# Hybrid retention and attention encoder layer with routed experts: order of the first expert weight blocks, residual input loaded elsewhere, and activations placed ahead of a weight split

## The reference

```python
def gated_merge(x, y_r, y_d, gr, gd, w_out):
    m = jax.nn.sigmoid(gr) * y_r + jax.nn.sigmoid(gd) * y_d
    return x + jnp.einsum('btd,de->bte', m, w_out)

def hier_moe(h, w_group, b_group, w_expert, b_expert, w_gate, w_up, w_down):
    ...
    for e in range(N_EXPERTS):
        he = jax.nn.silu(xt @ w_gate[e]) * (xt @ w_up[e])
        y = y + combine[:, e:e + 1] * (he @ w_down[e]).astype(F32)
    return y.reshape(B, T, D).astype(h.dtype)
```

## Time and profile before

| | us |
|---|---|
| median of 3 runs | 1039.63 (1039.24 to 1040.72) |
| profiled execution, its own time | 1038.06 |
| its span in the trace | 1036.2 |
| outside the span | 1.9 |
| mean granted TensorE clock | 0.996 |

### The profile page before, as it was taken

One profiled execution on the slowest core, in us unless ns is written; L12 is line 12 of the kernel. 1 busy time (PEld: TensorE's weight loads), 2 busy tenths in 40 slices (PEclk: granted clock), 3 DMA queues, 4 the chain that ended last, 5 costly groups with the idle time before them and its releaser, 6 DMA issues.

```text
span 1036.2 us, 12524 instructions
## 1 busy us (share of the span) xinstructions
PE 1011.0 (98%) x4814; PEld 834.1 (80%) x4814; DVE 679.0 (66%) x999; ACT 529.3 (51%) x728; POOL 149.8 (14%) x185
## 2 busy tenths in 40 slices
PE   7999999999999999999999999999999999999996
PEld 6888888887888878778778888888878888888774
DVE  6877765236566564344438556678799888888982
ACT  5433333435555555233352213455677877868772
POOL 1000020112111302111112000021121211212102
PEclk9999999999999999999999999999999999999998
DMA  9258855362542614432457433238899999999994
GB/s 302 83 193 302 306 202 193 126 242 94 192 164 91 207 59 162 163 113 106 168 183 265 151 107 134 102 107 317 316 422 384 404 382 404 394 393 404 382 391 65
DMA packets 62421, 237.69 MB, mean 229 GB/s; under 512 B 5632, under 2 KB 5936, under 8 KB 50032
## 3 DMA queue, kind: packets, MB, share of 16 engines
q1 hardware_dynamic: 41328, 162.80, 41.1%
q0 software_dynamic: 21024, 73.99, 21.6%
HBM read 199.40 MB, written 48.15 MB: 239 GB/s over the span
## 4 chain that ended last, share of the span: by engine, by line
PE 67%; issue 25%; POOL 3%; DVE 2%; ACT 1%; DMA 1%; POOLq 0%; SPq 0%; ACTq 0%; DVEq 0%
PE ps L472 16%; PE ps L474 16%; PE ps L473 16%; PE ps L1888 4%; PE ps L1889 4%; PE ps L1907 2%; PE ps L1857 2%; PE ps L1946 2%; POOL x_exp L835 1%; POOL out_y L846 1%; PE ps L2142 1%; PE ps L2042 1%; PE ps L2058 1%; PE ps L2049 1%; PE ps L1950 1%
## 5 line engine op out<-in xcount | busy, mean ns | idle before, releaser
L472 PE MATMUL ps<-w_hi,s_hi 128*128 128x512 f32 x672 | 267.0, 397 | 2.0 <-DVE w_lo L1352 1.8
L474 PE MATMUL ps<-w_lo,s_hi 128*128 128x512 f32 x672 | 262.3, 390 | 0.0
L473 PE MATMUL ps<-w_hi,s_lo 128*128 128x512 f32 x672 | 261.9, 390 | 0.0
L472 PEld LDWEIGHTS ps<-w_hi,s_hi 128*128 128x128 f32 x672 | 126.4, 188 | 28.1 <-DVE w_lo L1352 2.7
L474 PEld LDWEIGHTS ps<-w_lo,s_hi 128*128 128x128 f32 x672 | 126.2, 188 | 26.6
L473 PEld LDWEIGHTS ps<-w_hi,s_lo 128*128 128x128 f32 x672 | 126.4, 188 | 25.1 <-issue 0.2
L989 ACT ACTIVATE stage<-ps,x_rstd 128x512 f32<-128x512 f32 x64 | 43.9, 688 | 175.8 <-PE ps L474 175.4
L408 DVE TENSOR_TENSOR w_lo<-raw,w_hi 128x2048 fp32r<-128x2048 f32 x40 | 91.6, 2290 | 42.4 <-ACT w_hi L403 42.1
L403 ACT CAST w_hi<-raw 128x2048 fp32r<-128x2048 f32 x40 | 76.2, 1910 | 6.2 <-DMA raw<-in_w_out 3.5
L444 DVE TENSOR_TENSOR lo_x<-raw_x,w_hi 128x2048 fp32r<-128x2048 f32 x32 | 72.3, 2286 | 9.7 <-ACT w_hi L421 9.4
L444 DVE TENSOR_TENSOR lo_x<-raw_x,hi_x 128x2048 fp32r<-128x2048 f32 x32 | 72.2, 2287 | 8.7 <-ACT hi_x L421 8.6
(11 more groups left out here) (314 smaller groups left out, 1858.0 us busy)
## 6 DMA issues: line engine op xcount, KB each, us to landing
raw<-in_w_in SPq DMA_DIRECT2D x30, 1024.0 KB, 7.4
raw_x<-in_w_up SPq DMA_DIRECT2D x30, 1024.0 KB, 20.0
raw_x<-in_w_down SPq DMA_DIRECT2D x18, 1024.0 KB, 21.5
raw<-in_w_gate SPq DMA_DIRECT2D x16, 1024.0 KB, 19.1
raw_x<-in_w_gate SPq DMA_DIRECT2D x16, 1024.0 KB, 19.5
raw<-in_w_down SPq DMA_DIRECT2D x14, 1024.0 KB, 21.2
x_slots<-in_c_empty SPq DMA_DIRECT2D x4, 2112.0 KB, 16.6
x_exp<-x_slots POOLq DMA_DIRECT2D x16, 528.0 KB, 13.0
```

The lines of the kernel that those rows point to most:

```text
L472: nc.tensor.matmul(out, s_h, w_h, start=first, stop=False)
L473: nc.tensor.matmul(out, s_l, w_h, start=False, stop=False)
L474: return nc.tensor.matmul(out, s_h, w_l, start=False, stop=last)
```

## The change

Four things are changed together.

1. `RAW_ORDER` begins 6, 7, 2, 3, 0, 1, 4, 5. Blocks 0 and 1 go to slots 6 and 7, the SBUF of `gate[0]` and `gate[1]`, which are free once the first and second output products are taken (`p_evacuated` 5 and 10). Blocks 2 and 3 go where 0 and 1 went, blocks 4 and 5 where 2 and 3 went. So four blocks can be loaded before the routing instead of two. Blocks 6 and 7 go to slots 4 and 5, and the load of block 6 now waits for `x_loaded[1]`, the rows of expert 1 in SBUF. Block 8 waits for `row_ready` in place of both `x_loaded`; these two waits have moved to block 10. All later loads of SP stand behind these in its queue.
2. The residual is loaded to `res0` (tile 0) and into `rows_out`, tile by tile, when PE has transposed the tile that stood there.
3. The five stores of x2 stand behind blocks 0 to 3 instead of two on either side of blocks 2 and 3.
4. In `step`, on ACT and on DVE, the split of q = 8 stands behind `gate_silu` and `x_parts` (on DVE behind `gated` and `x_parts`), no longer ahead of them.

```diff
@@ -218,6 +218,7 @@
     gate_at = [X + 45056, X + 58880, X, X + 30720, X + 98304]
     gate = [at(f"gate{i}", [P, TT, COLS], f32, gate_at[i]) for i in range(5)]
+    res0 = [at("res00", [P, COLS], f32, X + 53248), at("res01", [P, COLS], f32, X + 67072)]
     gffn = at("gffn", [P, D_MODEL], f32, X + 40960)
     md, x2 = od, ro
@@ -327,7 +328,7 @@
     state_ready, state_evacuated, state_stored = sem("state_ready"), sem("state_evacuated"), sem("state_stored")
     src_ready, src_transposed = sem("src_ready"), sem("src_transposed")
     gate_in = [sem(f"gate_in{i}") for i in range(5)]
-    gate_opened = sem("gate_opened")
+    gate_opened, res_in = sem("gate_opened"), [sem(f"res_in{t}") for t in range(TT)]
     p_ready, p_evacuated = sem("p_ready"), sem("p_evacuated")
     wrs_ready, x2_squared, x2_rooted = sem("wrs_ready"), sem("x2_squared"), sem("x2_rooted")
     y_init, slots_empty = sem("y_init"), sem("slots_empty")
@@ -366,7 +367,7 @@
-    RAW_ORDER, HI_ORDER = [2, 3, 0, 1] + list(range(WR, RAW)), [2, 3, 0, 1] + list(range(WR, SPL))
+    RAW_ORDER, HI_ORDER = [6, 7, 2, 3, 0, 1, 4, 5] + list(range(SPL, RAW)), [2, 3, 0, 1] + list(range(WR, SPL))
     LAST = N0 - 2
     DENSE_LOADS = [len(range(r, LAST, WR)) for r in range(WR)] + [1, 1] + [0] * (RAW - WR - 2)
@@ -415,7 +416,7 @@
         if not isinstance(j, int) or m >= SPL:
             act.wait_ge(blocks_used, number(j, i, q) - SPL + 1)
         elif m < WR:
-            act.wait_ge(blocks_used, LAST - 1 + RAW_ORDER[m] if m >= 2 else LAST - 2)
+            act.wait_ge(blocks_used, LAST - 1 + HI_ORDER[m] if m >= 2 else LAST - 2)
         else:
             act.wait_ge(logits_ready, TT)
         nc.scalar.copy(hi_of(i, q), raw_of(i, q)).then_inc(hi_ready, 1)
@@ -579,16 +580,18 @@
             m = expert_block(i, q)
             if j is None and m < RAW:
                 if m < 2:
+                    sp.wait_ge(p_evacuated, TT * (m + 1))
+                elif m < WR:
                     sp.wait_ge(blocks_used, LAST - 2)
-                elif m < WR + 2:
-                    sp.wait_ge(blocks_used, LAST - 1 + m - 2)
-                elif m == 6:
-                    sp.wait_ge(p_evacuated, TT * OUT_CHUNKS - 1)
-                elif m == 7:
-                    sp.wait_ge(p_evacuated, TT * OUT_CHUNKS)
-                elif m == 8:
+                elif m < SPL:
+                    sp.wait_ge(blocks_used, LAST - 1 + m - WR)
+                    if m == WR + 2:
+                        sp.wait_ge(x_loaded[1], 16)
+                elif m == SPL:
                     sp.wait_ge(y_init, 16 * TT)
                     sp.wait_ge(sample_kept, 16)
+                    sp.wait_ge(row_ready, TT)
+                elif m == SPL + 2:
                     for k in range(2):
                         sp.wait_ge(x_loaded[k], 16)
             else:
@@ -610,12 +613,10 @@
             for i in range(NE):
                 for q, (kind, part) in enumerate((("w_up", 0), ("w_up", 1), ("w_gate", 0), ("w_gate", 1))):
-                    if j is None and i == 0 and q == 2:
-                        for t in ORDER[:PT]:
-                            keep_x2(t)
                     expert_load(j, i, q if i else 2 + q, i, kind, part)
                 if j is None and i == 0:
-                    keep_x2(ORDER[PT])
+                    for t in ORDER:
+                        keep_x2(t)
                 for part in range(2 if i else 0):
                     expert_load(j, i, 4 + part, i - 1, "w_down", part)
             for part in range(2):
@@ -690,11 +691,17 @@
         def load_gate(kind, half, i):
             c0 = half * COLS
-            if kind == "x":
-                dma(gate[i][:, 0:PT, :], tiles(a["x_prompt"][0], c0, c0 + COLS, 0, PT)).then_inc(gate_in[i], 16)
-                dma(gate[i][0:SAMPLE, PT, :], a["x_sample"][0][:, c0:c0 + COLS]).then_inc(gate_in[i], 16)
-            else:
-                dma(gate[i][:, :, :], tiles(z[kind], c0, c0 + COLS)).then_inc(gate_in[i], 16)
+            dma(gate[i][:, :, :], tiles(z[kind], c0, c0 + COLS)).then_inc(gate_in[i], 16)
+
+
+        def load_residual(t):
+            if t == 0:
+                for k in range(2):
+                    dma(res0[k][:, :], a["x_prompt"][0, 0:P, k * COLS:(k + 1) * COLS]).then_inc(res_in[0], 16)
+            elif t < PT:
+                dma(rows_out[:, t, 0:D_MODEL], a["x_prompt"][0, t * P:(t + 1) * P, :]).then_inc(res_in[t], 16)
+            else:
+                dma(rows_out[0:SAMPLE, t, 0:D_MODEL], a["x_sample"][0]).then_inc(res_in[t], 16)
         for c, (kind, _, c0) in enumerate(SECTION[0:PURE]):
@@ -807,10 +814,11 @@
         dma(w_r[:, :, NG:NG + NE], a["w_expert"][0].rearrange("(k p) c -> p k c", p=P)).then_inc(router_in, 16)
         pool.wait_ge(src_ready, 2 * TT)
         load_gate("gr", 1, 2)
-        pool.wait_ge(p_evacuated, TT)
-        load_gate("x", 0, 0)
         pool.wait_ge(p_evacuated, 2 * TT)
-        load_gate("x", 1, 1)
+        load_residual(0)
+        for t in range(1, TT):
+            pool.wait_ge(src_transposed, source_unit(3, t) + 2)
+            load_residual(t)
         pool.wait_ge(slots_empty, 16 * (NG + 1))
@@ -1248,12 +1256,12 @@
         def step(j, i, last=False):
             e = NE * j + i
             act_hi(i - 1, e - 1)
-            for q in (6, 7) if last else (6, 7, 8):
+            for q in (6, 7):
                 split_hi(act, j, i, q)
             gate_silu(j, i, e)
             if not last:
                 x_parts(i + 1, e + 1)
-                for q in (9, 10, 11):
+                for q in (8, 9, 10, 11):
                     split_hi(act, j, i, q)
             if last:
                 act_hi(i, e)
@@ -1589,11 +1597,8 @@
             if p == 0:
                 dve.wait_ge(gate_opened, k + 1)
                 return gate[k]
-            if p == 1:
-                dve.wait_ge(gate_in[4 if k == 0 else 2], 16 if k == 0 else 32)
-                return gate[4 if k == 0 else 2]
-            dve.wait_ge(gate_in[k], 48)
-            return gate[k]
+            dve.wait_ge(gate_in[4 if k == 0 else 2], 16 if k == 0 else 32)
+            return gate[4 if k == 0 else 2]
         def router_weights():
             dve.wait_ge(router_in, 80)
@@ -1611,9 +1616,13 @@
                 own(sum_halves(out_unit(x, t) % 2, IN_CHUNKS + x))
             else:
                 wait_out(dve, x, t)
-            gate_x = open_gates(p, k)
             rows, cols = slice(0, P if t < PT else SAMPLE), slice(k * COLS, (k + 1) * COLS)
-            g_t, out = gate_x[rows, t, :], md[rows, t, cols]
+            out = md[rows, t, cols]
+            if p < 2:
+                g_t = open_gates(p, k)[rows, t, :]
+            else:
+                dve.wait_ge(res_in[t], 32 if t == 0 else 16)
+                g_t = rows_out[rows, t, cols] if t else res0[k][:, :]
             product_t = ps[rows, out_unit(x, t) % 2, :] if t < PT else fold[:, :]
             if p == 0:
                 v.tensor_tensor(out, product_t, g_t, ALU.mult).then_inc(p_evacuated, 1)
```

## The result

The changed kernel takes 1042.15 us (median of 17 runs, 1039.7 to 1043.71), against 1039.45 us for the kernel before beside it (17 runs, 1038.27 to 1044.97). The medians lie 2.7 us apart; the ratio of the runs is 1.0019, or 2.0 us, with a 95% interval of 1.0010 to 1.0027, which is 1.0 to 2.8 us. The forecast was +1.5 us and a median of 1041.1 in a range of 1038.8 to 1043.4. The profiled execution took 1042.66 us, with a span of 1040.8.

A forecast was written before the change was run, and what follows sets the result against it. The prediction took the landing of the last weights, not PE, as the bound. Stream: +4.9 - 2.2 - 1.3 = +1.5 us, with PE's +2.1 and -2.0 hidden under it; 1039.63 + 1.5 = 1041.1 us, range 1038.8 to 1043.4.

The forecast's parts named there:

- The end is set by when the last weights land: End of the pass: landing of the last weights, not PE, sets it; after 1017.46 only 18.7 us of fixed work follow.
- The sum of the stream: Weight stream: +4.9 us for two held blocks, -2.2 from sooner scatters, -1.3 from not waiting for expert 0's rows; ends 1.5 later.
- the scatters' wait: POOL after its last scatter: wait falls from 5.10 to the quiet 2.94 us, so expert 1's rows load 2.2 us sooner.
- The -1.3 for expert 0's rows: SP ahead of the weight stream: waiting only for expert 1's rows, it issues at 738.3 rather than 739.56.
- PE at expert 1: The hold starts `up_gate(1)` 2.1 us later, at about 746.8; activations first give back 2.0 us, `up_gate(2)` at 765.5.
- rival 4: Block 6 lands at 746, not 741; PE 7.1 us behind at expert 1; +3.3 us, 1042.9; chance 0.06.
- block 7 lands 2.5 us later: Start of the held stream: block 6 lands at 741.0, block 7 at 743.5, its cast ending at 745.4.
- Late in the pass: New order removes most of PE's 1.8 us idle time in the last window; PE reaches expert 15's `act_t` some 2 us early.
- Rival 1: Scatters not sooner: the 5.10 us wait is theirs, stream starts only 1.3 us earlier; +3.6, 1043.3; chance 0.16 with halfway points.
- Rival 2: Even turns between DMA queues: the last scatter gains only 1.3 us from the missing weights; +2.3, 1041.9; chance 0.10.
- the prediction's paragraph on the queues: POOL's loads wait behind SP's backlog (8.6 us against 4.0); even turns, half the bandwidth, would add 1.3 us, not 4.6.
- The rest at nothing: Four early blocks and the residual in six loads before the experts cost nothing; early blocks gain nothing either.

The follow-up runs named there:

- acts_first: Kernel before with only the activation order changed (split of q = 8 behind the activation and next rows, ACT and DVE); 1039.35 us, ratio 1.0003.
- the two relatives: Kernel before with only block 6's wait for expert 1's rows added, and changed kernel with old step order; 1041.36 and 1041.03 us.
- hold8: Changed kernel with the hold moved from block 6 to block 8, which waits for expert 1's rows alone; 1039.19 us, ratio 0.9995.
- hold_only: Kernel before with only the hold added: block 6 waits for expert 1's rows; 1041.36 us, ratio 1.0016.
- old_steps: Changed kernel with the old order of the steps on ACT and DVE; 1041.03 us, ratio 1.0017.
- disp6: Changed kernel, but block 6 waits for all scatters to have landed, not expert 1's rows; block 10 waits for the rows; 1039.21 us, ratio 0.9999.
- hold5: Changed kernel with the hold one block earlier, at block 5, so three blocks are held; 1043.87 us, ratio 1.0040.
- no_hold: Changed kernel without the hold of block 6; block 8 goes as soon as the last rows are routed; 1039.43 us, ratio 0.9997.
- no_hold_late8: Changed kernel without the hold at block 6, block 8 waiting for both experts' rows as before; 1040.35 us, ratio 1.0000.
- disp8: Changed kernel without block 6's hold; block 8 waits for all scatters landed, block 10 for expert 1's rows; 1038.73 us (0.9991), again 1039.85 us (1.0003).
- disp7: Changed kernel, block 6 free; block 7 waits for all scatters landed, block 10 for expert 1's rows; 1039.34 us, ratio 1.0002.

## Why the prediction was right, and where it was off

*What sets the end.* "The end is set by when the last weights land": right. acts_first takes 1.6 us of waiting out of PE's path (`up_gate(2)` starts 2.1 us sooner, forecast 2.0) and the end stays within 0.02 us; in the changed kernel PE starts `up_gate(2)` 2.9 us later and the end moves by 1.4.

*The sum of the stream, +4.9 - 2.2 - 1.3 = +1.5.* Measured in the stretch: +1.4, and +1.8 in the two relatives. Term by term, with 3.19 us taken off the changed kernel's times: the scatters' wait 3.02 us, forecast 2.94; the rows' load issued at 732.27, forecast 731.95; block 6 issued at 736.13, forecast 736.1. The -1.3 for expert 0's rows, for which SP no longer waits, is in hold8: block 8 issued 1.27 us sooner, the stretch 1.2 shorter. The timed difference, +2.0 us (1.0 to 2.8), is 0.6 more than the stretch shows and 0.2 more than the way from 618 us does; the interval takes in all three.

*PE at expert 1.* Block 6 was cast at 741.1, forecast 741.0, which rules out rival 4. The step that was off is "block 7 lands 2.5 us later": its cast began 3.75 us after that of block 6. The start of a stream isn't its mean rate; the 2.5 came from a window of 20 us. The same two casts are 3.6 to 4.0 us apart for the first two held blocks of hold_only, old_steps, disp6 and hold5 too. So the rows were cast at 746.65, not 745.4, and PE started `up_gate(1)` at 748.13, +3.4 us and not +2.1. What delayed block 7, no run separates. Then came what the prediction did not have at all: the slower clock after the wait, 8 matmuls over 3.51 us, 0.2 apart too much each, 1.6 us. `up_gate(2)` was 2.9 us late and not 0.1 (771.47 and 765.40 from the two first casts). None of it reached the end: the stream was 1.4 us later too, and the rest came out of time that PE had lost to waits before. From the start of `up_gate(2)` to being ready for `acts_in(15)` PE took 252.06 us before and 248.68 in the change; the 1.8 us of idle time in the late window is only a part of these 3.4. That the two misses on PE's path (1.3 and 1.6 us) did not show in the result is owed to this slack, of which the prediction had counted 1.8 us.

*Late in the pass.* Forecast: hardly any idle time and some 2 us in hand ahead of `acts_in(15)`; measured 100.00 of 100 us, and 1.87 us. The reason that I gave for the first, a split of 2.2 us off the way to `act_t`, was wrong: acts_first has that and keeps its 1.6 us. It is the hold that takes the idle time away: hold_only, with the old order, has PE busy in 99.75 of the 100 us. PE then runs later against the landings.

*Rival 1*, scatters that gain nothing, fell with 3.02, 3.02, 3.02, 3.02 and 3.03 us in five kernels with at most one of the blocks 6 and 7 ahead of them. *Rival 2*, even turns between the queues: the turns are there, and the price is wrong, the rival's and that of the prediction's paragraph on the queues. This is what the two queues moved from 726 to 728 us in the kernel before (packets, MB, share of the 16 engines), SyncE's queue first and GpSimd's second:

```profile
q1 hardware_dynamic: 75, 0.61, 72.8%
q0 software_dynamic: 74, 0.25, 30.2%
```

Counted in packets they take even turns. But a packet of the weights is 8.1 KB here and one of the scatters 3.4, so GpSimd gets 0.25 of 0.86 MB, and not the half that both texts took. Even halves would have let 1.08 MB of scatters (two of 528 KB) pass at half of 425 GB/s, 2.5 us more than the quiet 3.0, so 5.5; with four blocks ahead, no_hold's last scatters waited 9.51 us, 190 packets of each queue passed from 733 to 738 us, and the pair of scatters before them was itself still on its way when they were issued. The Trainium skill, "DMA: Bandwidth & Descriptors", section on queues, rings and completion order, has an engine take turns packet by packet; counted so, these rows agree.

*The rest at nothing*: right, as far as no_hold_late8 tells (1.1 us either way); old_steps and hold_only differ by 0.01 us in the stretch, and ahead of the experts the way is the same within 0.1 us in all traces but the changed kernel's.

*The chances.* I gave 0.62 to a change within 0.2% and 0.32 to slower. It came out at +0.19%, just inside that border of 2.1 us, and the interval (0.10 to 0.27%) reaches over it on both sides: that it fell on this side was luck.

## What to carry to other kernels

Where a stream of weights sets the end, price a hold by the bytes that it moves from idle queues into the full stream, less what the work behind it starts sooner; holding two blocks cost 4.9 us (2.1 MB at 425 GB/s) and got 3.4 back, and the third cost 3.2 more and got nothing back. Before a load is sent sooner, look for the next wait behind it: blocks 8 and 9 went out up to 13 us earlier, and block 10, held by rows that the early weights themselves delayed, took it back. When two queues share the DMA engines, compare the size of their packets and not only their bytes. And an engine that is 98% busy may still not be the bound: 1.6 us saved on it turned into a wait of 1.7 ahead of its last stage.

## What the runs showed of the hardware

*A wait of 4 us halved PE's clock for the work behind it.* After 4.15 us without a matmul in the changed kernel, they started 0.43 us apart for 3.5 us, which is the 1.2 GHz level of its clock (512 columns in 0.427 us), and then 0.23 us apart again; the window's granted clock is 0.91. Waits of 2.5 us in no_hold (granted clock 0.79 from 744 to 752) and 2.7 us in disp8 (0.79 from 742 to 750) did it too, while the waits of 0.7 us in the kernel before and of 1.1 us in disp7 left it at 1.00 from 742 to 750. So the 4.15 us cost PE about 1.6 more. The Trainium skill, "TensorE: Matmul & The Clock Gate", Part 1 on the clock gate, has PE at the one level after idle time and back at the other after sustained work; these rows agree.

*What POOL issues beside SP's weights starts late and then gets even turns by packets, which is about a third of the bytes.* A 528 KB load of rows takes 4.0 us alone, with its first packets about 1.1 us after its issue. Beside weights, its first packets came 3.5 us after the issue (the kernel before, issued at 744.51) and 4.0 us (disp7, issued at 733.51), and from then on the two queues moved about the same number of packets (disp7, 738 to 744 us: 218 of POOL's and 222 of SP's, 0.85 and 1.69 MB); the loads took 8.6 us and a median of 10.5. Why the start is late, no run separates. The wait for the last scatters grows in the same way, by the blocks of 1.05 MB sent since 714 us beyond the first two: none 3.02 us, one 3.02 (disp7), two 4.6 to 5.7, four 9.51. One block did not lengthen the wait, though two did: in disp7 SP's queue moved only one packet more after 728 us, when the last pair of scatters was issued, and in the kernel before 29 after 728 and 75 in the 2 us before.
